# Moving yields and a square root in the RWKV stage of a two-block network

## The reference, cut to what matters

```
r, k, v, xw, xa, xg = split(cols + (token_shift(cols) - cols) * mu)
decay = exp(-exp(-softplus(-(w0 + tanh(xw) @ w2)) - 0.5))
a = sigmoid(a0 + xa @ a2);   g = sigmoid(xg) @ g2
kk = k * k_k;  kk = kk / max(norm(kk), 1e-12)
k = k * (1 + (a - 1) * k_a)
y = wkv7_scan(r, decay, k, v, -kk, kk * a)       # 4 heads of 64, 512 steps
o_b = (group_norm(y) + bonus(r, k, v)) * g @ w_o
merged = sigmoid(gate0) * (attention @ mla_w_o) + sigmoid(gate1) * o_b + sigmoid(gate2) * o_c
```

## Time and profile before

| | us |
|---|---|
| median of 3 runs | 3925.82 |
| lowest and highest | 3917.54, 3929.76 |
| the profiled execution's own time | 3917.54 |
| its span in the trace | 3915.5 |
| PE busy | 3738.2 |
| DVE, ACT, POOL busy | 1874.2, 1334.0, 479.6 |
| granted PE clock, mean | 0.981 |

### The profile page before, as it was taken

One profiled execution on the slowest core, in us unless ns is written; L12 is line 12 of the kernel. 1 busy time (PEld: TensorE's weight loads), 2 busy tenths in 40 slices (PEclk: granted clock), 3 DMA queues, 4 the chain that ended last, 5 costly groups with the idle time before them and its releaser, 6 DMA issues.

```text
span 3915.5 us, 52740 instructions
## 1 busy us (share of the span) xinstructions
PE 3738.2 (95%) x21400; PEld 2923.9 (75%) x21400; DVE 1874.2 (48%) x2908; ACT 1334.0 (34%) x1989; POOL 479.6 (12%) x392
## 2 busy tenths in 40 slices
PE   7889899999999999999999999999999999999999
PEld 3555668888887887788776767788877676778887
DVE  4555555434345655444455455443334445544333
ACT  4333333313134333322434432332233543233222
POOL 2221201000003212000112320000021132000000
PEclk9999999999999999999999999999999999999999
DMA  6323422221113232223211210233222121023331
GB/s 208 96 88 119 136 81 66 65 65 65 65 44 92 89 101 97 77 96 108 72 54 45 82 52 28 84 97 97 93 77 63 41 80 49 28 84 96 97 97 65
DMA packets 327345, 317.03 MB, mean 81 GB/s; under 512 B 8960, under 2 KB 312480, under 8 KB 327104
## 3 DMA queue, kind: packets, MB, share of 16 engines
q1 hardware_dynamic: 327104, 313.68, 25.5%
HBM read 311.55 MB, written 2.10 MB: 80 GB/s over the span
## 4 chain that ended last, share of the span: by engine, by line
PE 84%; DVE 8%; ACT 4%; issue 1%; DMA 1%; POOL 1%; DVEq 0%; ACTq 0%; SPq 0%; POOLq 0%
PE PS L133 83%; DVE scr L147 3%; ACT scr L143 2%; PE PS L136 1%; DVE scr L153 1%; DMA scr<-in_ada_w 1%; DVE scr L157 1%; DMA ring<-in_w_in 1%; ACT NBt L143 1%; ACT L143 1%; DVE NBt L157 1%; DVE scr L177 1%; DVE scr L165 1%; DVE PS L161 0%; DVE na_l L157 0%
## 5 line engine op out<-in xcount | busy, mean ns | idle before, releaser
L133 PE MATMUL PS<-scr 128*32 128x32 f32 (+11 forms) x6812 | 625.6, 285 | 76.0 <-DVE scr L147 27.8
L133 PEld LDWEIGHTS PS<-scr 128*32 128x32 f32 (+4 forms) x6812 | 458.7, 150 | 238.8 <-issue 126.3
L133 PE MATMUL PS<-ffn_h,ffn_w 128*128 128x512 f32 (+1 forms) x3024 | 589.1, 357 | 4.0 <-DVE ffn_h L157 3.6
L133 PEld LDWEIGHTS PS<-ffn_h,ffn_w 128*128 128x128 f32 x3024 | 502.6, 190 | 90.5 <-issue 5.2
L143 ACT ACTIVATE scr<-PS 128x256 f32<-128x256 f32 (+4 forms) x437 | 199.9, 458 | 645.7 <-PE PS L133 565.1
L143 ACT ACTIVATE scr<-scr 128x256 f32<-128x256 f32 (+7 forms) x390 | 192.8, 494 | 502.2 <-DVE scr L157 314.7
L133 PE MATMUL PS<-mlp_h,mlp_w 128*128 128x512 f32 x1536 | 359.7, 395 | 0.0
L133 PE MATMUL PS<-mlp_g,mlp_w 128*128 128x512 f32 x1536 | 358.0, 395 | 0.0
L133 PE MATMUL PS<-h_h,ring_r 128*128 128x512 f32 (+1 forms) x976 | 341.6, 413 | 5.9 <-DVE scr L165 3.8
L133 PEld LDWEIGHTS PS<-mlp_h,mlp_w 128*128 128x128 f32 x1536 | 288.8, 188 | 68.5 <-issue 1.0
L133 PEld LDWEIGHTS PS<-mlp_g,mlp_w 128*128 128x128 f32 x1536 | 289.0, 188 | 67.7
(11 more groups left out here) (174 smaller groups left out, 4814.3 us busy)
## 6 DMA issues: line engine op xcount, KB each, us to landing
ring<-in_ffn_w_in SPq DMA_DIRECT2D x44, 1024.0 KB, 5.1
scr<-in_ada_w SPq DMA_DIRECT2D x52, 768.0 KB, 4.7
ring<-in_w_up SPq DMA_DIRECT2D x32, 1024.0 KB, 5.5
ring<-in_w_down SPq DMA_DIRECT2D x32, 1024.0 KB, 5.0
ring<-in_w_in SPq DMA_DIRECT2D x60, 512.0 KB, 3.9
ring<-in_ffn_w_out SPq DMA_DIRECT2D x16, 1024.0 KB, 5.0
scr<-in_na_bias SPq DMA_DIRECT2D x32, 512.0 KB, 5.0
ring<-in_na_w_qkv SPq DMA_DIRECT2D x24, 512.0 KB, 4.1
```

The source lines that it names most:

```text
L133: return self.eng.matmul(o, lhsT=l, rhs=r, start=start, stop=stop) if self.eng else Nothing()
```

## The change

It has five parts. (1) PE: one of three yields between the transposes of v and those of a and k goes. (2) ACT: the two square roots move from turn n = 7, behind the halving of the merge's tile 0 (in layer 1 of the tile rv1), to the end of turn n = 6. (3) ACT: the yield between the exponentials and the copies of the transposes goes. (4) DVE: one of the yields behind c_ar goes and the other moves ahead of it; c_ar and the bonus now stand in one round. (5) POOL: seven empty yields become six. Each chain now has six yields where it had seven, so the merge makes 21 steps beside the chain instead of 24. No computation is added or removed.

```diff
@@ rw_pe, chain()
                 if j == 0:
                     yield
                     yield
-                    yield
@@ rw_act
             halve_act(act, ...)
-            for i in range(2):
-                if n == 7:
-                    act.wait_ge(*at("rw_in", "kn_r", l, i))
-                    act.f(rtm[i], rtm[i], ACT.Sqrt)...
             act.wait_ge(*at("rw_full", l, n))
             act.f(C[:, n, 1:513], psum("rw_made", "r_c", l, n), ACT.Copy)...
             for i in range(2):
                 if n == 4:
                     ...
+                elif n == 6:
+                    act.wait_ge(*at("rw_in", "kn_r", l, i))
+                    act.f(rtm[i], rtm[i], ACT.Sqrt)...
@@ rw_dve, chain()
             yield
+            yield
             dve.wait_ge(*at("rw_made", "ec", l, 1))
             (c_ar)
-            yield
-            yield
             (bonus)
@@ rw_pool, chain()
-            for _ in range(7):
+            for _ in range(6):
```

More of the change, by code:

```diff
@@ L3260, in rw_act @@
             halve_act(act, *((1024, "rw", l, n + 1) if n < 7 else (256, "rv1") if l else (1024, "mg", l, 0, 0)))
-            for i in range(2):
-                if n == 7:
-                    act.wait_ge(*at("rw_in", "kn_r", l, i))
-                    act.f(rtm[i], rtm[i], ACT.Sqrt).then_inc(*act.up("rw_made", "kn_rs", l, i))
             act.wait_ge(*at("rw_full", l, n))
@@ L3270, in rw_act @@
                     act.f(rtm[i], kk[:, i, :], ACT.Square).then_inc(*act.up("rw_made", "kk_sq", l, i))
+                elif n == 6:
+                    act.wait_ge(*at("rw_in", "kn_r", l, i))
+                    act.f(rtm[i], rtm[i], ACT.Sqrt).then_inc(*act.up("rw_made", "kn_rs", l, i))
         if l:
```

## The result

| | before | after |
|---|---|---|
| median, us | 3925.79 (5 runs) | 3953.97 (5 runs) |
| lowest and highest | 3917.54, 3929.76 | 3947.09, 3958.71 |
| the profiled execution's own time | 3917.54 | 3941.19 |
| its span | 3915.5 | 3939.1 |

The ratio is 1.0067 (95%: 1.005 to 1.0084). 3935 was predicted, 3921 to 3946 the range: the time lies above it. The traces differ by 23.6 us, the medians by 28.2. The profiled execution of after is faster than all five that its median is taken from, so its trace shows less than the usual loss.

The account below looks back on a forecast made before the run. PE was taken as the bound (84% of the chain ending last). Loop starts +3.6 and −0.9 us plus 3.7 per loop for deferred merge work made +10.1, 3935.9 against the median, given as 3935; range 3921 to 3946.

Parts of the forecast that it names:

- six products, layer 0: PE's six products in layer 0's chain start 2.0 us later, behind a new wait of 2.7 us for merge tile 0.
- loop start, layer 0: Layer 0's loop starts 3.6 us later, at 2300.0, or 0.8 later if POOL does not disturb DVE.
- loop start, layer 1: Layer 1's loop starts 0.9 us earlier, at 3271.5, or 3.7 earlier if POOL does not disturb DVE.
- Deferred work: Three merge steps, 5.0 us per layer, leave the chain and cost 3.7 us in each loop, bounds 0 and 5.0.
- Roots: Moved roots delay tile 0's halving: PE waits 2.7 us in layer 0, six products +2.0; layer 1 nothing, at most 1.
- Copies ahead of the sigmoid: On ACT in layer 0, copies delay group 1's sigmoid; PE starts gate tile 2 at 2278.1, 3.3 us later.
- POOL's disturbance of DVE in c_ar: Three POOL operations beside DVE's c_ar lengthen it by 0.95 us each, 2.85 in all, bounds 0 and 2.85.
- the rival without it (3930): Rival: POOL doesn't disturb DVE's c_ar, sum +4.5 us, time 3930; chance 0.18.
- The waits for c_ar: PE waits for DVE just ahead of the 16 transposes, 5 us in layer 0 and 5.6 in layer 1.
- The 1.80 of the earlier trace: PE's wait in layer 1 ahead of mo of group 2, for DVE's product of group 1, 1.80 us, goes for certain.
- swallow the merge: Rival: 5.0 us more merge filler costs the loop nothing; with POOL out of c_ar's way −2.9 us, 3923; chance 0.16.
- late first copies: Rival: ACT's first loop copies stand behind gate tile 4's transfer; each layer loses about 2 us, 3940; chance 0.16.

Follow-up runs that it names:

- the roots only: The kernel before with only the two ACT square roots moved ahead of the halving of merge tile 0: 3938.34 us, ratio 1.0022 to before.
- seven yields: After with one more empty yield at the end of each chain, so nothing is deferred and the new orders stay: 3947.83 us, ratio 1.0056 to before.
- shift only: Before with only the six yields, so three merge steps go from chain to loop; roots, copies and c_ar ordered as before: 3932.02 us, ratio 1.0014.
- roots back: After with the two square roots put back behind the halving of merge tile 0: 3947.98 us, ratio 1.0049 to before.
- orders back: After with the old order of copies on ACT and c_ar on DVE, six yields and moved roots kept: 3933.59 us, ratio 1.0028 to before.
- a third of a step: 0.34 merge steps per loop turn instead of 0.5: after 3935.63 us (1.0023 to before), shift only 3919.32 (0.9978), before 3924.07 (0.9992).
- the kernel with roots and fillings: Before with the roots moved and ten and twelve unread PE products in two waits of layer 0: 3931.26 us, ratio 1.0008 to before.

## Why the prediction was wrong

**What failed: a new wait was priced at its own length.** "A new wait of 2.7 us. The eighteen products then end at 2251.8 + 4.3" and "transposes ... make 12.5" took the work behind each wait at the speed it had before, and so did the 3.7 us for each loop. The clock stood at nothing in the sum, without a reason given. Some of that work ran at 1.2 GHz. Point by point, in the two traces:

| step | predicted | measured | of it the clock |
|---|---|---|---|
| six products, layer 0 | +2.0 | +3.8 | 1.6 (18 products 5.9 for 4.3) |
| from there to the end of c_ar | +1.5 beyond these | +2.0 | |
| end of c_ar to the loop, layer 0 | 12.5 long | 14.3 | 1.8 |
| loop start, layer 0 | +3.6 | +7.5 | 3.4 |
| loop, layer 0 | +3.7 | +7.9 | about 3.7 |
| loop start, layer 1 | −0.9 | +1.7 | 2.2 (14.7 for 12.5) |
| loop, layer 1 | +3.7 | +4.2 | none |
| sum | +10.1 | +21.3 | about 9.3 |

In the last column 3.4 is the sum of the two rows above it, and 9.3 of 1.6, 1.8, 3.7 and 2.2. "About 3.7" is what layer 0's loop has beyond layer 1's, and is put down to the two stretches at 2353.0 and 2380.3, half of which is 3.4. So the clock is most of the 11.2 us by which the two stages miss the sum. Of the 19 us between 3935 and 3954 it is about half; 2.3 more lie in stretches of the trace where nothing was changed, some 4.6 in the distance of the medians beyond that of the traces, and about 1 in the rounding from 3935.9 to 3935. Without the clock's 9.3 the stages would give +12.0 for +10.1: the orders, the waits and the deferral were priced nearly right.

That the clock is the cause is shown for the chain: with unread products in the waits the same work behind them ran at 1.00 (5.4 us less in after's trace, 2.8 in the one with the roots only), and behind one and the same wait of 2.69 eighteen products took 5.90 us or 4.33, as the clock fell or not. For the loop it is read from the traces and not shown by an experiment of its own.

The Trainium skill, in "TensorE: Matmul & The Clock Gate", section "Part 1: The HAM clock gate", says that the slow level is the default and activity releases it. The traces agree in the main: the windows behind after's waits had 0.50 to 0.91, and 1.00 where unread products stood in them; but behind a wait of 2.69 with seven yields the windows had 1.00 too.

**Deferred work.** 5.0 us left the chain: right (5.0 and 4.4 in shift only). Its price of 3.7 per loop is right for the work itself: 4.2 in the loop of layer 1 of after, which has no further slow stretch, and 2.1 to 4.5 in the eight loops of after, roots back, orders back and shift only, when half of their slow time beyond 3.4 us is taken off (an estimate). The loops grew by 4.2 to 10.4, as some had up to 17 us of slow stretches. The earlier trace rows are of a loop with 3.4 us and could not show that. It was also not weighed that the price hangs on how thinly the work is spread.

**Roots.** Mechanism and wait right: 2.69 us for POOL's half, forecast 2.7; nothing in layer 1. The step's size of 2.0 was 3.8 with the clock, and 2.2 with seven yields, where the clock stayed full; alone in before the roots cost 5.3. The load took 1.28 us and the root began 0.01 later, so the drain of some 1.38 us that the Trainium skill has in "ScalarE: Activation LUTs", section "What ACT_TABLE_LOAD costs", does not show here either, and leaving it out was right.

**Copies ahead of the sigmoid, c_ar, POOL.** Right. Gate tile 2 at 2281.79 is 2278.1 with 1.9 of offset and 1.8 from the roots' step. POOL's disturbance of DVE in c_ar was 3.0 us, forecast 2.85; the rival without it (3930) is out. The waits for c_ar were 3.93 and 5.71 (5 and 5.6; of the first the eighteen products ahead of it, slow now, hid 1.4). The 1.80 of the earlier trace rows are gone.

**Rivals.** The loop did not swallow the merge: every loop of a kernel with six yields and half a step is 4.2 us or more longer than before's. (the earlier trace rows has only the waits for DVE; PE also waited 2.2 us for ACT there.) The late first copies came in part, and with the shift, not with the new orders (PE waited 1.91 there in shift only): in after ACT waited 7.24 us for the transfer of gate tile 4 and then halved it from 2306.13 on, and PE waited 1.68 ahead of 2310.29; but with a third of a step the loops of after fell to 169.8 and 168.0 while that wait was 1.82, so it does not set the loop's length.

**What stays open.** After's medians lie 28 us above before's, the trace shows 23.6, of which the two stages hold 21.3. The mean granted clock is known for every execution: of the fifteen of after the profiled one has the highest, 0.979, the middle ones of about 3953 us have 0.973 and the slowest, 3960.85, 0.971; before has 0.981 in its trace and 0.978 at 3926.53, its median in a later series. So more time at 1.2 GHz is part of what the medians lie apart beyond the traces; where it falls no trace shows. In other traces more slow stretches lie in the loops where nothing at all was changed: the kernel with roots and fillings has one of 6.8 and one of 10.2 us in layer 1's loop (176.3 long for 169.1). Why they fall in one execution and not in another was not settled.

## What to carry to other kernels

Where PE is the bound and runs at its full clock, price a new wait of PE at its length, and for the case that the clock falls at its length plus what PE loses at half speed behind it, here 1.6 to 2.2 us more for waits of 2.7 to 5.7. The clock fell at the wait of 2.7 in three traces and not in two others. If such a wait can't be avoided, products that nobody reads may cost less than the wait. When work is moved into a loop, look how evenly it lies there before pricing it by the microsecond: with six yields, half a step or a third of a step per turn made 14 us; with seven, no difference that could be told from none.

## What had not been expected of the hardware

- A wait of 2.14 us was followed by full clock in one kernel and by 1.2 GHz in another (2274.75 in before, 2281.70 with the roots only), and so was one of 2.69 (2254.03 with seven yields, 2253.78 in after): the same wait has two prices.
- 56 products more made the kernel faster, by 12.6 us (4 to 21), of which 5.4 are found in the chains of the trace.
- c_ar's float32 operations with two inputs in SBUF took 1.47 us each beside POOL (5.89 for four) and 0.71 without it, while POOL's two on the ring took 3.26, and 2.65 in the earlier trace rows: both took longer, DVE far more.
